# The FFNs' normalised activations, moved 320 bytes along the partition

## The chip, the cores and the metric

One core of one Trainium2 chip. The metric is device time in microseconds (us) for the whole program, weights read from HBM included; the time quoted is the median of three runs. The profile comes from one more execution, taken by the hardware profiler.

## What is computed

Two transformer blocks on 256 tokens of width 1024, all in fp32 (depth 1 each). The first has a mixer over 272 tokens (16 meta tokens in front) and an FFN, the second has an FFN, a mixer and another FFN. What matters here are the three FFNs, each of the form

```python
def swiglu(x, w_in, w_out):
    gate, up = jnp.split(x @ w_in, 2, axis=-1)
    return (jax.nn.silu(gate) * up) @ w_out

x = x + FFN_RESIDUAL_SCALE * rmsnorm_2(swiglu(rmsnorm_2(x, pre), w_in, w_out), post)
```

with an inner width of 2816 (11 groups of 256 columns). In the first block the FFN is the same without the norm behind it and without the factor.

## The kernel before

**Precision.** Every large product is made of three products of fp32r matmuls: weights and activations are each split in a high part and a low part (`whi`, `wlo`; `xn` high, `xn` low), and what is summed in PSUM is whi by high, whi by low and wlo by high.

**Weights.** They come in 129 units of 128 partitions by 2048 values (8192 bytes a partition, 1 MB). SP's queue loads a unit into `raw` (3 slots), ScalarE (line 683) rounds it to `whi`, VectorE (line 1011) makes `wlo` from the two. The tensors `raw`, `whi` and `wlo`, three slots of 8192 bytes a partition each, are allocated one behind the other, and `xa` right behind them. A stationary operand is 128 columns of a unit (512 bytes a partition), so each begins a whole multiple of 512 bytes before the start of `xa`.

**Activations.** `xa` holds 8 times 544 values. For the four norms in front of the three FFNs and of the second mixer, `xn[k]` (k = 0, 1 and 3 for the FFNs, 2 for the mixer) is a view of `xa` in 8 k-tiles of 512 values (2048 bytes): 256 values of high part (one a token), then 256 of low part. The view begins at value `XN_AT[k]`:

```python
XN_AT = (0, 0, 80, 0)
xn = [xa_line[:, c:c + KT * 2 * SEQ].rearrange("p (k c) -> p k c", k=KT) for c in XN_AT]
```

So before the change the FFNs' moving operands begin at the weights' residue modulo 512 bytes, and those of the second mixer 320 bytes past it. ScalarE writes the high parts (line 729), VectorE the low ones (line 1022).

**An FFN on TensorE** (`ffn`, all matmuls issued through the helper `mm`, line 1466). `first_paired_unit` does the first gate unit: per k-tile and 128 columns, whi and wlo by the high part (256 wide), and at the end whi by the low part (256 wide), 48 matmuls. Then `up(0)`, and then ten times a group of gate, up and down:

- `gate`: `hi_products`, 16 matmuls 512 wide (whi by high and low side by side), then `lo_products`, 16 matmuls 256 wide (wlo by high)
- `up`: `lo_products`, then `hi_products`
- `down` (`rows_tile`): 24 matmuls 512 wide, in which the inner activations `hhi`, `hlo` are stationary and the weights move. They do not read `xa`

The last down unit is `rows_last_unit`, from `ya`. In `lo_products` and `hi_products` two matmuls in a row have the same moving operand and two stationary ones.

**The second mixer** uses the same `xa` at 80 values: `first_columns_unit` (48 matmuls 256 wide, in the order of `first_paired_unit`), `columns_tile` (per k-tile whi by high, whi by low, wlo by high, 256 wide) and `tokens_tile` (the activations stationary, the weights moving, 256 wide).

All order is written out by hand; engines meet through semaphores. TensorE waits for a unit's parts (`hi_ready`, `lo_ready`), for the PSUM banks to be read out (`gate_out`, `up_out`) and for the inner activations (`hlo_done`).

Of the kernel before, what the change touches and what calls it, by code (L numbers as in the profile page):

```python
# [45 lines left out]
GROUPS = FF // 256  # L46
UNIT = 2048
SLOTS = 3
XN_AT = (0, 0, 80, 0)
EPS = 1e-6  # L50
NEG = -1e30

# [217 lines left out]
def build_blocks(nc, x_in, meta_in, wstream, ident_in, vecs_in, small_in, const_in, rows_in, out):  # L270
    with ExitStack() as ctx:  # L271
# [146 lines left out]
        neg_sides = exact[:, C_AT["neg_before"][0]:C_AT["neg_after"][0] + P].rearrange("p (a b) -> p a b", a=2)  # L418
        since_r, ones_r = exactly("from"), exactly("ones")
        xa_line = xa[:].rearrange("p k c -> p (k c)")  # L420
        xn = [xa_line[:, c:c + KT * 2 * SEQ].rearrange("p (k c) -> p k c", k=KT) for c in XN_AT]
        ps_line = ps[:].rearrange("p b c -> p (b c)")

# [2 lines left out]
        def vec(name, i=0, n=1):  # L427
            return vecs[:, V_NORM[name] + i:V_NORM[name] + i + n]
# [241 lines left out]
        def _(act):  # L670
# [54 lines left out]
            def hi_of(k, gain, tiles):  # L725

                for kt in tiles:
                    act.wait_ge(norm_turned, KT // 2 + 4 * k + turn_group(kt) + 1)
                    nc.scalar.activation(xn[k][:, kt, 0:SEQ], turn_place(k, kt), ACT.Copy, scale=vec(gain, kt)).then_inc(xa_hi_ready, 1)

            def root_of_x(p, tt):

# [266 lines left out]
        def _(dve):  # L999
# [18 lines left out]
            def norm(k, gain):  # L1018
                for kt in range(KT):

                    dve.wait_ge(xa_hi_ready, KT * (k + 1) + 2 * turn_group(kt) + 2)
                    nc.vector.scalar_tensor_tensor(  # L1022
                        xn[k][:, kt, SEQ:2 * SEQ], turn_place(k, kt), vec(gain, kt),
                        xn[k][:, kt, 0:SEQ].bitcast(F32), ALU.mult, ALU.subtract).then_inc(xa_ready, 1)

                split_ahead(LAST[k])

# [436 lines left out]
        def _(pe):  # L1464
# [26 lines left out]
            def columns_tile(o, slot, a, of, n, skip=0):  # L1491

                for kt in range(KT):
                    w = slice(kt * 256 + a * P, kt * 256 + (a + 1) * P)
                    mm(o, whi[slot][:, w], of[:, kt, skip:n], kt == 0, False)
                    mm(o, whi[slot][:, w], of[:, kt, n + skip:2 * n], False, False)
                    ins = mm(o, wlo[slot][:, w], of[:, kt, skip:n], False, kt == KT - 1)
                return ins

            def first_paired_unit(bank, slot, k):  # L1500

                for kt in range(KT):
                    if k < 2 and kt == 2:
                        pe.wait_ge(x_written, X_BEFORE[k] + len(HALVES))
                        turn_raw(k, range(4, KT), range(TT), True)
                    pe.wait_ge(xa_hi_ready, KT * (k + 1) + kt + 1)
                    for a in range(2):
                        w = slice(kt * 256 + a * P, kt * 256 + (a + 1) * P)
                        mm(ps[:, bank + a, 0:SEQ], whi[slot][:, w], xn[k][:, kt, 0:SEQ], kt == 0, False)
                        mm(ps[:, bank + a, 0:SEQ], wlo[slot][:, w], xn[k][:, kt, 0:SEQ], False, False)  # L1510
                for kt in range(KT):
                    pe.wait_ge(xa_ready, KT * (k + 1) + kt + 1)
                    for a in range(2):
                        w = slice(kt * 256 + a * P, kt * 256 + (a + 1) * P)
                        ins = mm(ps[:, bank + a, SEQ:2 * SEQ], whi[slot][:, w], xn[k][:, kt, SEQ:2 * SEQ], False, kt == KT - 1)
                return ins

            def first_columns_unit(bank, slot, k):

                tiles = [(ps[:, bank, a * SEQ:(a + 1) * SEQ], a * P) for a in range(2)]
                for kt in range(KT):
                    pe.wait_ge(xa_hi_ready, KT * (k + 1) + kt + 1)
                    for o, c in tiles:
                        w = slice(kt * 256 + c, kt * 256 + c + P)
                        mm(o, whi[slot][:, w], xn[k][:, kt, 0:SEQ], kt == 0 and c == 0, False)  # L1530
                        mm(o, wlo[slot][:, w], xn[k][:, kt, 0:SEQ], False, False)
                for kt in range(KT):
                    pe.wait_ge(xa_ready, KT * (k + 1) + kt + 1)
                    for o, c in tiles:
                        w = slice(kt * 256 + c, kt * 256 + c + P)
                        ins = mm(o, whi[slot][:, w], xn[k][:, kt, SEQ:2 * SEQ], False, kt == KT - 1)
                return ins

            def tokens_tile(o, slot, tt):

                hi, lo = slice(tt * P, (tt + 1) * P), slice(SEQ + tt * P, SEQ + (tt + 1) * P)
                for kt in range(KT):
                    w = slice(kt * 256, (kt + 1) * 256)
                    mm(o, xn[2][:, kt, hi], whi[slot][:, w], kt == 0, False)
                    mm(o, xn[2][:, kt, hi], wlo[slot][:, w], False, False)
                    ins = mm(o, xn[2][:, kt, lo], whi[slot][:, w], False, kt == KT - 1)
                return ins

            def rows_tile(slot, a, act_hi, act_lo, first, last):
# [81 lines left out]
            for kind, i in FIRST:  # L1631
# [3 lines left out]
                if kind == "proj":  # L1635
                    n = U_IN + i // 2
                    query = IN_KIND[i][0] == "q"
                    if i == 0:
                        first_unit()
                    if i >= 2:  # L1640
                        pe.wait_ge(lo_ready, n + 1)
                        wait_tiles(pe, i - 2)
                        skip = META if query else 0
                        columns_tile(ps[:, i % 2, skip:TOK], n % SLOTS, i % 2, xa, TOK,
                                     skip).then_inc(unit_used if i % 2 else even_full, 1)
                if kind == "gates":

# [129 lines left out]
            def ffn(f):  # L1777
# [65 lines left out]
            for kind, i in SECOND:  # L1843
                if kind == "munit":
                    n, bank = U_MIX + i, UNIT_BANK[i]
                    pe.wait_ge(lo_ready, n + 1)
                    if i == N_MIX - 1:
                        pe.wait_ge(ml_turn_taken, 3)
                    elif i >= 2:
                        wait_taken(pe, i - 2)  # L1850
                    if i == 0:
                        ins = first_columns_unit(bank, n % SLOTS, 2)
                    elif MIX_KIND[i] == "v":
                        for tt in range(TT):
                            ins = tokens_tile(two(bank)[:, tt, :], n % SLOTS, tt)
                    else:
                        for a in range(2):
                            if (i, a) == (1, 1):

                                pe.wait_ge(mgate_out, 1)  # L1860
                                for tt in range(TT):
                                    c = SEQ + tt * 16
                                    ins = mm(ps[:, 2, c:c + 16], gate_halves[:, tt * P:(tt + 1) * P], vec("gate_sum", 0, 16)[0:BACK + 16, :],
                                             True, True)
                                ins.then_inc(mgate_done, 1)
                            ins = columns_tile(ps[:, bank, a * SEQ:(a + 1) * SEQ], n % SLOTS, a, xn[2], SEQ)
                    ins.then_inc(unit_used, 1)
                if kind == "mgates":
                    spread_rstd(2, 3)
                    pe.wait_ge(gate_w_ready, 1)  # L1870
                    for kt in range(KT):
                        for part in range(2):
                            ins = mm(ps[0:BACK + 16, 2, 0:SEQ], gate_w[:, kt, :], xn[2][:, kt, part * SEQ:(part + 1) * SEQ],
                                     kt == 0 and part == 0, kt == KT - 1 and part == 1)
# [140 lines left out]
```

## Time and profile before

| | |
|---|---|
| median of 3 runs | 797.41 us (797.29 to 797.64) |
| the profiled execution | 797.35 us |
| its span | 795.6 us |
| TensorE matmul busy | 785.1 us (99%), 4710 instructions |
| TensorE weight load busy | 693.8 us (87%) |
| VectorE, ScalarE, GpSimd busy | 533.2, 429.5 and 28.3 us |
| HBM read | 139.69 MB, 177 GB/s over the span |

The span is the time from the program's first instruction to its last; some 1.7 us of the execution lie around it. A matmul's recorded duration is its latency, longer than the step from its start to that of the next, since matmuls overlap: how fast TensorE goes is read from the starts.

### The profile page before, as it was taken

To read this page: it belongs to the slowest core of one execution; us is meant where nothing else is said; L and a number is where in the kernel's file an instruction comes from. 1 tells how busy PE (TensorE), PEld (TensorE's weight loads), DVE (VectorE), ACT (ScalarE), POOL (GpSimd) and SP (SyncE) were. 2 spreads that over 40 slices of the span, in tenths; PEclk is the share of its full clock that TensorE was granted. 3 is DMA by queue.
4 is the path that set the end of the run, shared out by engine and by line. 5 is a ranking of instruction groups with operands and counts; after the bars stand their busy time and mean duration, and the time that the engine had idled before them with its cause. 6 is when DMAs were issued, how large, how long until landed. Compare 5 with 4: busy or idle time off the path is not lost.

```text
span 795.6 us, 12209 instructions
## 1 busy us (share of the span) xinstructions
PE 785.1 (99%) x4710; PEld 693.8 (87%) x4710; DVE 533.2 (67%) x628; ACT 429.5 (54%) x565; POOL 28.3 (4%) x35
## 2 busy tenths in 40 slices
PE   9999999999999999999999999999999999999997
PEld 8989979888888888888888887999988888888885
DVE  7865567766666667866666566766977766666665
ACT  6556658444544548744544446565557644454444
POOL 0000000000000000000000000002420000000000
PEclk9999999999999999999999999999999999999999
DMA  9633333655555543665555554452444655555521
GB/s 335 232 115 117 140 110 139 229 182 187 205 172 203 184 185 110 238 227 192 202 171 208 180 189 158 140 204 108 160 167 165 218 217 175 194 198 175 208 105 54
DMA packets 20797, 141.16 MB, mean 177 GB/s; under 512 B 2448, under 2 KB 2704, under 8 KB 4384
## 3 DMA queue, kind: packets, MB, share of 16 engines
q1 hardware_dynamic: 20192, 138.65, 49.0%
q0 software_dynamic: 576, 2.10, 0.8%
q8 instruction: 21, 0.34, 0.2%
q14 instruction: 8, 0.07, 0.0%
HBM read 139.69 MB, written 1.05 MB: 177 GB/s over the span
## 4 chain that ended last, share of the span: by engine, by line
PE 94%; DVE 2%; ACT 2%; issue 1%; DMA 1%; SPq 0%; DVEq 0%; ACTq 0%
PE ps L1466 93%; ACT whi L683 1%; PE ps L1472 1%; DMA raw<-wstream 1%; DVE x L1215 0%; ACT squared L698 0%; DVE xa L1022 0%; PE ps L1695 0%; DVE wlo L1011 0%; PE ps L1665 0%; PE ps L1915 0%; DVE xg L1210 0%; DVEq L271 0%; ACT L916 0%; PE ps L1697 0%
## 5 line engine op out<-in xcount | busy, mean ns | idle before, releaser
L1466 PE MATMUL ps<-xa,whi 128*128 128x512 f32 (+2 forms) x1744 | 376.1, 346 | 0.0
L1011 DVE TENSOR_TENSOR wlo<-raw,whi 128x2048 fp32r<-128x2048 f32 x128 | 293.7, 2295 | 82.2 <-ACT whi L683 82.1
L1466 PEld LDWEIGHTS ps<-xa,whi 128*128 128x128 f32 x1744 | 300.2, 188 | 40.0 <-issue 2.1
L683 ACT ACTIVATE whi<-raw 128x2048 fp32r<-128x2048 f32 x128 | 244.1, 1908 | 6.9 <-PE ps L1466 6.8
L1466 PE MATMUL ps<-xa,wlo 128*128 128x256 f32 (+1 forms) x1376 | 225.7, 283 | 0.0
L1466 PEld LDWEIGHTS ps<-xa,wlo 128*128 128x128 f32 x1376 | 193.6, 191 | 2.4
L1466 PE MATMUL ps<-whi,hhi 128*128 128x512 f32 x240 | 93.4, 389 | 0.0
L1466 PE MATMUL ps<-wlo,hhi 128*128 128x512 f32 x240 | 93.4, 389 | 0.0
L1466 PE MATMUL ps<-whi,hlo 128*128 128x512 f32 x240 | 93.4, 389 | 0.0
L863 ACT ACTIVATE arena<-ps 128x512 f32<-128x512 f32 x33 | 19.7, 596 | 87.1 <-PE ps L1466 87.1
L877 ACT ACTIVATE hhi<-arena 128x512 fp32r<-128x512 f32 x30 | 19.0, 632 | 88.1 <-PE ps L1466 81.6
L871 ACT ACTIVATE arena<-ps 128x512 f32<-128x512 f32 x33 | 19.7, 596 | 74.1 <-PE ps L1466 74.1
L1466 PE MATMUL ps<-whi,ya 128*128 128x512 f32 x176 | 56.4, 394 | 0.0
L1466 PEld LDWEIGHTS ps<-wlo,hhi 128*128 128x128 f32 x240 | 45.0, 188 | 9.4
L1466 PEld LDWEIGHTS ps<-whi,hlo 128*128 128x128 f32 x240 | 45.0, 188 | 9.4
L1466 PEld LDWEIGHTS ps<-whi,hhi 128*128 128x128 f32 x240 | 45.0, 188 | 9.3
L1257 DVE TENSOR_TENSOR arena<-ps,arena 128x512 f32<-128x512 f32 x33 | 22.8, 691 | 41.1 <-ACT arena L863 41.1
L1266 DVE TENSOR_TENSOR arena<-ps,arena 128x512 f32<-128x512 f32 x33 | 22.8, 691 | 39.3 <-ACT arena L871 39.3
L1278 DVE TENSOR_TENSOR hlo<-arena,hhi 128x512 fp32r<-128x512 f32 x30 | 20.8, 694 | 37.4 <-ACT hhi L877 37.4
L1466 PEld LDWEIGHTS ps<-whi,ya 128*128 128x128 f32 x176 | 33.0, 188 | 6.8
L1466 PE MATMUL ps<-wlo,ya 128*128 128x512 f32 x88 | 34.6, 393 | 0.0
L1466 PE MATMUL ps<-arena 64*128 64x144 f32 (+11 forms) x190 | 23.9, 337 | 1.7 <-DVE arena L1055 1.3
(221 smaller groups left out, 531.5 us busy)
## 6 DMA issues: line engine op xcount, KB each, us to landing
raw<-wstream SPq DMA_DIRECT2D x128, 1024.0 KB, 4.8
gain_row<-rows_in POOLq DMA_DIRECT2D x4, 512.0 KB, 3.9
x<-x_in SPq DMA_DIRECT2D x2, 512.0 KB, 4.0
raw<-wstream SPq DMA_DIRECT2D x2, 512.0 KB, 5.6
out<-x SPq DMA_DIRECT2D x4, 256.0 KB, 2.1
xg<-const_in SPq DMA_DIRECT2D x1, 912.0 KB, 13.0
small<-small_in SPq DMA_DIRECT2D x1, 152.0 KB, 6.0
arena<-meta_in SPq DMA_DIRECT2D x1, 64.0 KB, 4.6
```

The source lines that it names most:

```text
L683: nc.scalar.activation(whi[slot][:], raw[slot][:], ACT.Copy).then_inc(hi_ready, 1)
L863: nc.scalar.activation(silu, products(4)[1], ACT.Copy).then_inc(gate_lo_out, 1)
L871: nc.scalar.activation(up_sum, products(6)[1], ACT.Copy).then_inc(up_lo_out, 1)
L877: nc.scalar.activation(ya[:, 0:2, 0:SEQ] if last else hhi[:], hact, ACT.Copy).then_inc(hhi_done, 1)
L1011: nc.vector.tensor_tensor(wlo[slot][:], raw[slot][:], whi[slot][:].bitcast(F32), ALU.subtract).then_inc(lo_ready, 1)
L1257: nc.vector.tensor_tensor(silu, products(4)[0], silu, ALU.add).then_inc(gate_out, 1)
L1266: nc.vector.tensor_tensor(up_sum, products(6)[0], up_sum, ALU.add).then_inc(up_out, 1)
L1278: nc.vector.tensor_tensor(lo, hact, hi.bitcast(F32), ALU.subtract).then_inc(hlo_done, 1)
L1466: return nc.tensor.matmul(o, lhsT, rhs, start=start, stop=stop, skip_group_check=True)
L1472: ins = nc.tensor.transpose(turn_place(k, kt)[:, tt * P:(tt + 1) * P], x[:, tt, kt * P:(kt + 1) * P], ident[:])
```

## The change

All four views now begin at value 80, so the FFNs' moving operands stand 320 bytes on from where they were, as the mixer's did. The views are cut by part (`xn_hi`, `xn_lo`) instead of by columns; with `XN_HI` all 0 and the distance between the parts `SEQ`, the parts lie beside each other as before, and the 512-wide operand is still 512 values in a row. The order of instructions on every engine, their shapes and their waits stay the same. What differs in the program is the offset of `xa` in the FFNs' instructions: 1152 matmuls 256 wide and 1008 matmuls 512 wide as executed, and the 24 writes of each part on ScalarE and VectorE. (`columns_tile` and `tokens_tile` take their operands in another form, with the same addresses.)

```diff
-XN_AT = (0, 0, 80, 0)
+XN_AT = ((80, SEQ),) * 4
+XN_HI = (0, 0, 0, 0)
...
-        xn = [xa_line[:, c:c + KT * 2 * SEQ].rearrange("p (k c) -> p k c", k=KT) for c in XN_AT]
+
+        xn = []
+        for at, far in XN_AT:
+            line = xa_line[:, at:at + KT * 2 * SEQ if far == SEQ else at + 2 * far]
+            if far == SEQ:
+                xn.append(line.rearrange("p (k h c) -> p k h c", k=KT, h=2))
...
+        xn_hi = [xn[k][:, :, n, :] for k, n in enumerate(XN_HI)]
+        xn_lo = [xn[k][:, :, 1 - n, :] for k, n in enumerate(XN_HI)]
...
-                    nc.scalar.activation(xn[k][:, kt, 0:SEQ], turn_place(k, kt), ACT.Copy, scale=vec(gain, kt)).then_inc(xa_hi_ready, 1)
+                    nc.scalar.activation(xn_hi[k][:, kt, :], turn_place(k, kt), ACT.Copy, scale=vec(gain, kt)).then_inc(xa_hi_ready, 1)
...
-                        xn[k][:, kt, SEQ:2 * SEQ], turn_place(k, kt), vec(gain, kt),
-                        xn[k][:, kt, 0:SEQ].bitcast(F32), ALU.mult, ALU.subtract).then_inc(xa_ready, 1)
+                        xn_lo[k][:, kt, :], turn_place(k, kt), vec(gain, kt),
+                        xn_hi[k][:, kt, :].bitcast(F32), ALU.mult, ALU.subtract).then_inc(xa_ready, 1)
...
-                            ins = mm(ps[:, bank + a, :], whi[slot][:, w], xn[norm][:, kt, 0:2 * SEQ], start and kt == 0, not start and kt == KT - 1)
+                            ins = mm(two(bank + a), whi[slot][:, w], xn[norm][:, kt, :, :], start and kt == 0, not start and kt == KT - 1)
...
-                            ins = mm(ps[:, bank + a, 0:SEQ], wlo[slot][:, w], xn[norm][:, kt, 0:SEQ], start and kt == 0, not start and kt == KT - 1)
+                            ins = mm(ps[:, bank + a, 0:SEQ], wlo[slot][:, w], xn_hi[norm][:, kt, :], start and kt == 0, not start and kt == KT - 1)
```

## Rows read from the trace of the kernel before

**Rows 1.** The page: busy time, share of the span, instructions; the chain that ended last

```profile
PE 785.1 (99%) x4710; PEld 693.8 (87%) x4710; DVE 533.2 (67%) x628; ACT 429.5 (54%) x565; POOL 28.3 (4%) x35
...
PE 94%; DVE 2%; ACT 2%; issue 1%; DMA 1%; SPq 0%; DVEq 0%; ACTq 0%
```

**Rows 2.** What TensorE waited for: us in total, times, longest us

```profile
PE ps L1472 <- DVE x L1215: 2.8, 4, 0.9
PE ps L1466 <- DVE arena L1055: 1.3, 1, 1.3
```

**Rows 3.** TensorE's groups by shape: xcount | busy us, mean ns of one | idle before

```profile
L1466 PE MATMUL ps<-xa,whi 128*128 128x512 f32 x1008 | 240.0, 390 | 0.0
L1466 PE MATMUL ps<-xa,wlo 128*128 128x256 f32 x1264 | 195.2, 282 | 0.0
L1466 PE MATMUL ps<-xa,whi 128*128 128x256 f32 x512 | 93.7, 283 | 0.0
```

**Rows 4.** Timeline of one group of the first FFN: start us, us to last end

```profile
154.64 3.79 PE L1466 MATMUL ps<-xa,whi 128*128 128x512 f32 x16
158.27 4.00 PE L1466 MATMUL ps<-xa,wlo 128*128 128x256 f32 x32
162.10 3.82 PE L1466 MATMUL ps<-xa,whi 128*128 128x512 f32 x16
165.76 0.39 PE L1466 MATMUL ps<-whi,hhi 128*128 128x512 f32 x1
...
171.20 3.79 PE L1466 MATMUL ps<-xa,whi 128*128 128x512 f32 x16
```

**Rows 5.** The first FFN's first units, timeline (offset 0)

```profile
127.48 0.28 PE L1466 MATMUL ps<-xa,whi 128*128 128x256 f32 x1
...
130.12 2.08 PE L1466 MATMUL ps<-xa,whi 128*128 128x256 f32 x16
132.03 2.08 PE L1466 MATMUL ps<-xa,wlo 128*128 128x256 f32 x16
133.96 2.23 PE L1466 MATMUL ps<-xa,whi 128*128 128x512 f32 x9
```

**Rows 6.** The second mixer's first unit, timeline (offset 80)

```profile
498.04 0.28 PE L1466 MATMUL ps<-xa,whi 128*128 128x256 f32 x1
...
501.44 1.98 PE L1466 MATMUL ps<-xa,whi 128*128 128x256 f32 x16
```

**Rows 7.** The second mixer, half of its unit 1, timeline (`columns_tile`, offset 80)

```profile
506.14 0.40 PE L1466 MATMUL ps<-xa,whi 128*128 128x256 f32 x2
...
508.85 0.28 PE L1466 MATMUL ps<-xa,wlo 128*128 128x256 f32 x1
```

**Rows 8.** Matmuls with `xa` in six stretches (by tile): duration ns min/median/max, first and last start

```profile
L1466 PE MATMUL ps<-xa,wlo x29: 278/283/283, 158.3 to 161.6; 128*128 128x256 f32 x29
...
L1466 PE MATMUL ps<-xa,wlo x16: 276/276/276, 497.9 to 501.3; 128*128 128x256 f32 x16
...
L1466 PE MATMUL ps<-whi,xa x29: 281/281/363, 512.9 to 517.9; 128*128 128x256 f32 x29
...
L1466 PE MATMUL ps<-whi,xa x29: 276/276/276, 519.9 to 524.6; 128*128 128x256 f32 x29
...
L1466 PE MATMUL ps<-xa,whi x28: 279/280/280, 532.9 to 537.7; 128*128 128x256 f32 x28
...
L1466 PE MATMUL ps<-xa,whi x15: 389/389/389, 154.6 to 157.8; 128*128 128x512 f32 x15
```

**Rows 9.** Weight loads in three of these stretches, same columns

```profile
L1466 PEld LDWEIGHTS ps<-xa,wlo x28: 188/192/192, 158.4 to 161.6; 128*128 128x128 f32 x28
...
L1466 PEld LDWEIGHTS ps<-xa,wlo x15: 187/188/188, 498.0 to 501.2; 128*128 128x128 f32 x15
...
L1466 PEld LDWEIGHTS ps<-xa,whi x14: 187/188/188, 154.9 to 157.8; 128*128 128x128 f32 x14
```

**Rows 10.** Last matmuls with `ya` before TensorE waits: duration, same columns

```profile
L1466 PE MATMUL ps<-whi,ya x2: 388/388/389, 493.3 to 493.5; 128*128 128x512 f32 x2
```

**Rows 11.** Busy us of engines in the four stretches of rows 4's group, clock, DMA

```profile
core 0: us, PE busy (x) PEld busy (x) DVE busy (x) ACT busy (x) POOL busy (x), PEclk, DMA share, GB/s
...
154.64:158.27 3.63, 3.63 (x18) 3.00 (x16) 1.59 (x2) 2.44 (x2) 0.00 (x0) 1.00 0.80 284
158.27:162.10 3.83, 3.83 (x33) 3.83 (x32) 2.45 (x3) 1.72 (x2) 0.00 (x0) 1.00 0.30 75
162.10:165.76 3.66, 3.66 (x19) 3.01 (x18) 2.62 (x2) 1.20 (x2) 0.00 (x0) 1.00 0.51 215
165.76:171.20 5.44, 5.44 (x26) 4.50 (x25) 3.67 (x3) 2.40 (x2) 0.00 (x0) 1.00 0.51 193
```

**Rows 12.** ScalarE writes the high parts of one norm, timeline

```profile
606.56 3.03 ACT L729 ACTIVATE xa<-ps,vecs 128x256 fp32r<-128x256 f32 x8 [1.35 <-PE ps L1472]
```

More of the change, by code:

```diff
@@ L420, in build_blocks @@
         xa_line = xa[:].rearrange("p k c -> p (k c)")
-        xn = [xa_line[:, c:c + KT * 2 * SEQ].rearrange("p (k c) -> p k c", k=KT) for c in XN_AT]
+        xn = []
[3 more added lines that the diff above has]
+                xn.append(line.rearrange("p (k h c) -> p k h c", k=KT, h=2))
+            else:
+                xn.append(line.rearrange("p (h r) -> p h r", h=2)[:, :, 0:KT * SEQ].rearrange("p h (k c) -> p k h c", k=KT))
+        xn_hi = [xn[k][:, :, n, :] for k, n in enumerate(XN_HI)]
+        xn_lo = [xn[k][:, :, 1 - n, :] for k, n in enumerate(XN_HI)]
+        xa_hi, xa_lo = xa[:, :, 0:TOK], xa[:, :, TOK:2 * TOK]
         ps_line = ps[:].rearrange("p b c -> p (b c)")
@@ L1489, in spread_rstd, with columns_tile @@
                 ins.then_inc(rstd_spread, 1)
-            def columns_tile(o, slot, a, of, n, skip=0):
+            def columns_tile(o, slot, a, of_hi, of_lo, skip=0):
                 for kt in range(KT):
                     w = slice(kt * 256 + a * P, kt * 256 + (a + 1) * P)
-                    mm(o, whi[slot][:, w], of[:, kt, skip:n], kt == 0, False)
-                    mm(o, whi[slot][:, w], of[:, kt, n + skip:2 * n], False, False)
-                    ins = mm(o, wlo[slot][:, w], of[:, kt, skip:n], False, kt == KT - 1)
+                    mm(o, whi[slot][:, w], of_hi[:, kt, skip:], kt == 0, False)
+                    mm(o, whi[slot][:, w], of_lo[:, kt, skip:], False, False)
+                    ins = mm(o, wlo[slot][:, w], of_hi[:, kt, skip:], False, kt == KT - 1)
                 return ins
@@ L1508, in first_paired_unit @@
                         w = slice(kt * 256 + a * P, kt * 256 + (a + 1) * P)
-                        mm(ps[:, bank + a, 0:SEQ], whi[slot][:, w], xn[k][:, kt, 0:SEQ], kt == 0, False)
-                        mm(ps[:, bank + a, 0:SEQ], wlo[slot][:, w], xn[k][:, kt, 0:SEQ], False, False)
+                        mm(ps[:, bank + a, 0:SEQ], whi[slot][:, w], xn_hi[k][:, kt, :], kt == 0, False)
+                        mm(ps[:, bank + a, 0:SEQ], wlo[slot][:, w], xn_hi[k][:, kt, :], False, False)
                 for kt in range(KT):
@@ L1514, in first_paired_unit @@
                         w = slice(kt * 256 + a * P, kt * 256 + (a + 1) * P)
-                        ins = mm(ps[:, bank + a, SEQ:2 * SEQ], whi[slot][:, w], xn[k][:, kt, SEQ:2 * SEQ], False, kt == KT - 1)
+                        ins = mm(ps[:, bank + a, SEQ:2 * SEQ], whi[slot][:, w], xn_lo[k][:, kt, :], False, kt == KT - 1)
                 return ins
@@ L1529, in first_columns_unit @@
                         w = slice(kt * 256 + c, kt * 256 + c + P)
-                        mm(o, whi[slot][:, w], xn[k][:, kt, 0:SEQ], kt == 0 and c == 0, False)
-                        mm(o, wlo[slot][:, w], xn[k][:, kt, 0:SEQ], False, False)
+                        mm(o, whi[slot][:, w], xn_hi[k][:, kt, :], kt == 0 and c == 0, False)
+                        mm(o, wlo[slot][:, w], xn_hi[k][:, kt, :], False, False)
                 for kt in range(KT):
@@ L1535, in first_columns_unit @@
                         w = slice(kt * 256 + c, kt * 256 + c + P)
-                        ins = mm(o, whi[slot][:, w], xn[k][:, kt, SEQ:2 * SEQ], False, kt == KT - 1)
+                        ins = mm(o, whi[slot][:, w], xn_lo[k][:, kt, :], False, kt == KT - 1)
                 return ins
             def tokens_tile(o, slot, tt):
-                hi, lo = slice(tt * P, (tt + 1) * P), slice(SEQ + tt * P, SEQ + (tt + 1) * P)
+                t = slice(tt * P, (tt + 1) * P)
                 for kt in range(KT):
                     w = slice(kt * 256, (kt + 1) * 256)
-                    mm(o, xn[2][:, kt, hi], whi[slot][:, w], kt == 0, False)
-                    mm(o, xn[2][:, kt, hi], wlo[slot][:, w], False, False)
-                    ins = mm(o, xn[2][:, kt, lo], whi[slot][:, w], False, kt == KT - 1)
+                    mm(o, xn_hi[2][:, kt, t], whi[slot][:, w], kt == 0, False)
+                    mm(o, xn_hi[2][:, kt, t], wlo[slot][:, w], False, False)
+                    ins = mm(o, xn_lo[2][:, kt, t], whi[slot][:, w], False, kt == KT - 1)
                 return ins
@@ L1643, in _ @@
                         skip = META if query else 0
-                        columns_tile(ps[:, i % 2, skip:TOK], n % SLOTS, i % 2, xa, TOK,
+                        columns_tile(ps[:, i % 2, skip:TOK], n % SLOTS, i % 2, xa_hi, xa_lo,
                                      skip).then_inc(unit_used if i % 2 else even_full, 1)
@@ L1865, in _ @@
                                 ins.then_inc(mgate_done, 1)
-                            ins = columns_tile(ps[:, bank, a * SEQ:(a + 1) * SEQ], n % SLOTS, a, xn[2], SEQ)
+                            ins = columns_tile(ps[:, bank, a * SEQ:(a + 1) * SEQ], n % SLOTS, a, xn_hi[2], xn_lo[2])
                     ins.then_inc(unit_used, 1)
@@ L1871, in _ @@
                     for kt in range(KT):
-                        for part in range(2):
-                            ins = mm(ps[0:BACK + 16, 2, 0:SEQ], gate_w[:, kt, :], xn[2][:, kt, part * SEQ:(part + 1) * SEQ],
-                                     kt == 0 and part == 0, kt == KT - 1 and part == 1)
+                        mm(ps[0:BACK + 16, 2, 0:SEQ], gate_w[:, kt, :], xn_hi[2][:, kt, :], kt == 0, False)
+                        ins = mm(ps[0:BACK + 16, 2, 0:SEQ], gate_w[:, kt, :], xn_lo[2][:, kt, :], False, kt == KT - 1)
                     ins.then_inc(mgate_halves, 1)
```

## The prediction

> **What bounds the kernel now.** I read the page first. TensorE is busy 99% of the span, the other engines 67% and less, and 94% of the chain that ended last runs through TensorE [rows 1]. The list of TensorE's waits comes next: its longest entries are 2.8 and 1.3 us in 795.6 [rows 2]. The timeline of one FFN group then gives the steps, as differences of starts [rows 4]: the 16 matmuls of gate's `hi_products` take 158.27 - 154.64 = 3.63 us, 227 ns each; the 32 of the two `lo_products` 3.83 us, 119.7 ns each; up's 16 of `hi_products` 3.66 us, 0.03 us more than gate's; the 24 of `down` 5.44 us, 226.7 ns each. Nothing else stands between them: 16.56 us a group, all of it matmul steps.
>
> **What a 256-wide matmul costs at either offset.** At offset 0 the first units show 120.0 ns (22 steps from 127.48 to 130.12) and 120.6 ns for the `lo_products` of `up(0)` (132.03 to 133.96, 16 steps) [rows 5]. At offset 80 the mixer's first unit, which runs through its k-tiles in the same order as `first_paired_unit`, shows 3.40 us for 30 steps, 113.3 ns [rows 6]. The durations say the same: 283 ns against 276 ns [rows 8], and the weight loads beside them 192 ns against 188 ns [rows 9]. But the mixer doesn't always get that: `columns_tile` at the same offset takes 2.71 us for 23 steps, 117.8 ns [rows 7], with durations of 279 to 280 ns. Of the two `tokens_tile` units, equal in all but the slot and the bank, one has 281 ns and the other 276 ns [rows 8]. So offset 80 has two steady paces, 113.3 and 117.8 ns, and which one a stretch falls into isn't set by the offset alone. I take 113.3 for the FFNs, for two reasons: their loops have two stationary operands in a row on one moving operand, as `first_columns_unit` has and `columns_tile` hasn't; and no wait of TensorE precedes them within a group. 117.8 stays as the other end.
>
> **What a 512-wide matmul costs.** The trace has none with `xa` at offset 80; it is the open price of this change. I take no change, 226.7 ns. For it: the weight load beside the 512-wide matmuls already has the undisturbed 188 ns at offset 0 [rows 9]; 226.7 is twice the undisturbed 113.3 of the half width; and the last 512-wide matmuls before a wait of TensorE, with no load behind them, still last 388 ns against 389 [rows 8, 10], so the load costs them next to nothing. Bounds from rows: 6.7 ns less a matmul, if they carry what the 256-wide ones carry (120.0 - 113.3), and 4.5 ns more, if they fall into the slower of the two paces (117.8 - 113.3).
>
> **The sum.**
> - Ten groups in each of three FFNs: 32 x (119.7 - 113.3) = 0.205 us, and the 0.03 us that up's `hi_products` carry over from the disturbed stream before them. 0.235 x 30 = 7.05 us.
> - `up(0)`, three times: 16 x (120.6 - 113.3) + 30 = 147 ns, 0.44 us.
> - `first_paired_unit`, three times: of 48 matmuls some 46 steps at 120.0 - 113.3, 0.31 us, 0.9 us.
> - 1008 matmuls 512 wide [rows 3]: nothing. Of the other rows of that group, 1056 of the 1264 and 96 of the 512 are the 1152 just counted; the rest belong to the mixers and keep their addresses.
> - `down`, the last units, both mixers: not touched.
> - The writes on ScalarE and VectorE at other addresses: nothing. ScalarE makes a k-tile's high part in about 0.36 us (eight in 3.03, of some 0.48 each, overlapped) [rows 12], and TensorE would use one in 4 x 113.3 = 453 ns, instead of 480.
>
> All of it lies on TensorE's path: 8.4 us. Does the cover hold? In the group VectorE is busy 10.3 us and ScalarE 7.8 us of 16.56 (sums of the four stretches, rows 11), and the DMA engines are no more than 0.80 busy in any of them; a group of 16.32 us leaves all of them room, and no new wait comes first. The profiled execution took 797.35 us, 0.06 under the median of the runs, so 797.35 - 8.4 = **789.0 us**.
>
> **The rivals.**
>
> *The slower of the two paces.* The 256-wide matmuls fall to 117.8 ns only. Then 960 x 1.9 + 48 x 2.8 + 138 x 2.2 = 2.3 us, and up to 1.0 us of carry-over: 794.5 us. For it: ten of the second mixer's twelve units run at this pace, with durations of 279 to 281 ns (three of them in rows 7 and 8). Against it: the order of the FFNs' loops, and that gate's `lo_products` come out of a stretch at 226.7.
>
> *The 512-wide ones gain as well.* If an undisturbed matmul costs a fixed 6.7 ns beside its columns, whatever its width, then 226.7 is 213.3 + 6.7 and another 6.7 of disturbance, and 1008 x 6.7 = 6.8 us go too: 782.2 us. For it: 120.0 is 106.7 + 6.7 + 6.7 by the same count. Against it: the 388 ns with no load beside it [rows 10]. If a width costs nothing but its columns, a 512-wide matmul would last 276 + 106.7 = 383 ns, and it lasts 388. In this direction points the Trainium skill, page "TensorE: Matmul & The Clock Gate", section "Back-to-back issue gap", which has 518 cycles for 512 columns, 215.8 ns at 2.4 GHz. By that, an estimate, the 512-wide matmuls would have up to 11 us to give; no stretch of this trace shows them under 226.
>
> *Slower: the 512-wide ones are thrown out of step.* They stream twice as long as the load, and in the whole trace they run undisturbed only where both operands stand at the same residue (`hi_products` and `down` alike). Moved by 320 bytes, each takes the 4.5 ns of the slower pace: 1008 x 4.5 = 4.5 us, in `gate` and `up` of all groups. With the 256-wide ones at 117.8 the sum is 797.35 - 2.3 + 4.5 = 799.6 us, slower. It decides the sign from 2.3 ns a matmul on. Should the 256-wide ones reach 113.3, the same loss leaves 793.4, still faster. Against it: the first 107 ns of such a matmul, in which the load runs, are those of a 256-wide one, and these are undisturbed at offset 80 [rows 6].
>
> *The offset does nothing.* The 113.3 of rows 6 then come from that unit's place in the program (slot 2, one bank, what ScalarE and VectorE do beside it) and not from the 320 bytes: 797.35 us. For it: equal units of the mixer differ by as much [rows 8]. Against it: in the FFNs slots 0, 1 and 2, banks 4 to 7 and all loads on the other engines come by, and the pace is 119.4 to 120.6 everywhere. This is also what the Trainium skill, page "SBUF — State Buffer", section "Who interferes with whom", would have: TensorE has two independent read ports there, for the moving operand and the weight load, and "PE and ACT never wait on anyone". The trace has 276 and 283 ns for one shape, which that rule doesn't explain.
>
> **How the numbers follow.** A measurement of this kernel tells about 0.2%, 1.6 us, from no change. The forecast has 0.50 (788 to 790), the slower pace 0.20, the gain of the 512-wide ones 0.10, their loss 0.10, no effect 0.10. The first three are faster: 0.80; no effect 0.10; slower 0.10. The predicted time is that of the likeliest case. The range leaves out the two cases of the 512-wide matmuls, 0.20 together, and reaches from under the forecast (786.5, should some of the 512-wide ones gain) to no change (797.6).
>
> **What would show it.** Right: one group's `lo_products` x32 take 3.63 us from start to start, with durations of 276 ns and loads of 188; up's `hi_products` 3.63 instead of 3.66; `first_paired_unit` 113.3 ns a step; gate's 16 wide ones 3.63 and `down` 5.44 as before; a group 16.32 us. The slower pace shows as 3.77 us and 279 to 281 ns. The 512-wide matmuls show a loss as 3.70 us for 16 and a gain as 3.52. The prediction is wrong if the 512-wide steps move by more than 1 ns in either direction, if the 256-wide ones stay above 115, or if TensorE's waits grow by the time saved.

## The result, and the profile after

The changed kernel takes 793.92 us (median of 5 runs, 793.66 to 793.95) against 797.64 us (5 runs) for the kernel before: a ratio of 0.995, 95% interval 0.9937 to 0.9963. That is 3.7 us, of the 8.4 us that were forecast (789.0). The sign was right, the size wrong by more than half.

The page of the changed kernel has the same engine shares as [rows 1], with TensorE's busy time down by 3.5 us and the span at 792.0 us (795.6 before):

```profile
PE 781.6 (99%) x4710; PEld 687.9 (87%) x4710; DVE 533.2 (67%) x628; ACT 429.3 (54%) x565; POOL 28.3 (4%) x35
...
PE 94%; ACT 2%; DVE 2%; issue 1%; DMA 1%; SPq 0%; DVEq 0%; ACTq 0%
```

In the steady groups no wait took the time over. What TensorE waited for (us in total, times, longest) is as in [rows 2], with 0.5 us at a place that had 0.3:

```profile
PE ps L1484 <- DVE x L1227: 2.8, 4, 0.9
PE ps L1478 <- DVE arena L1067: 1.3, 1, 1.3
PE ps L1478 <- DVE arena L1101: 0.5, 1, 0.5
```

(Lines stand 12 further down in the changed file: `mm` is at 1478.) The groups by shape (count | busy us, mean ns) already show both signs: against [rows 3] the narrow matmuls with wlo last 5 ns less, the wide ones 2 ns more, and the ones of `down`, which don't read `xa`, have a mean of 390 (389 before).

```profile
L1478 PE MATMUL ps<-xa,whi 128*128 128x512 f32 x1008 | 241.7, 392 | 0.0
L1478 PE MATMUL ps<-xa,wlo 128*128 128x256 f32 x1264 | 189.3, 277 | 0.0
L1478 PE MATMUL ps<-wlo,hhi 128*128 128x512 f32 x240 | 93.5, 390 | 0.0
```

The same group of the first FFN as in [rows 4], timeline, start and length in us:

```profile
154.77 3.84 PE L1478 MATMUL ps<-xa,whi 128*128 128x512 f32 x16
158.45 3.79 PE L1478 MATMUL ps<-xa,wlo 128*128 128x256 f32 x32
162.08 3.82 PE L1478 MATMUL ps<-xa,whi 128*128 128x512 f32 x16
...
171.19 3.84 PE L1478 MATMUL ps<-xa,whi 128*128 128x512 f32 x16
174.87 3.79 PE L1478 MATMUL ps<-xa,wlo 128*128 128x256 f32 x32
```

From start to start: gate's 16 wide matmuls 3.68 us (3.63 before), the 32 narrow ones 3.63 (3.83), up's 16 wide ones with the 24 of `down` 9.11 (9.10). A group takes 16.42 us, not 16.32. The durations (min/median/max) say which kind is disturbed: the narrow ones have the clean 276 ns of [rows 8] throughout, the wide ones now scatter from 388 to 394 where all had 389.

```profile
L1478 PE MATMUL ps<-xa,wlo x28: 276/276/276, 158.6 to 161.6; 128*128 128x256 f32 x28
...
L1478 PE MATMUL ps<-xa,whi x13: 388/392/394, 155.2 to 158.0; 128*128 128x512 f32 x13
```

Where the 0.133 us of a group come from, by the steps from one matmul's start to the next in the steady groups (ns, differences of starts, divided by their count):

| kind | before | after | in a group |
|---|---|---|---|
| 32 narrow, xa by wlo | 119.8 | 113.3 | -206 ns |
| 16 wide of gate, behind `down` | 226.7 | 230.1 | +54 ns |
| 16 wide of up, behind narrow ones | 228.4 | 228.7 | +5 ns |
| 24 of `down` | 226.7 | 227.2 | +13 ns |
| a group | 16553 | 16420 | -133 ns |

27 such intervals make 3.6 us. The first units and the first group of an FFN gain almost nothing (in the first FFN from 127.16 to 154.64 before, from 127.38 to 154.77 after: 0.1 us; 0.1 and 0.0 us in the other two). There the narrow ones of the first group run at 117.8 ns:

```profile
141.85 3.93 PE L1478 MATMUL ps<-xa,wlo 128*128 128x256 f32 x32
```

And `first_paired_unit` is faster, but in the first and the third FFN TensorE then meets a wait that it did not have. `up(0)` needs the `wlo` that VectorE makes meanwhile. Before, VectorE was done with it at 131.80 us (129.52 + 2.28) and TensorE came to it at 132.03 [rows 5]; now VectorE is done at 132.02 and TensorE starts at 132.07, with 0.17 us more in the two steps around that start than at the pace beside them (0.1 us in the third FFN). The list of waits doesn't have it, since matmuls before it are still recorded as running.

```profile
129.52 2.28 DVE L1011 TENSOR_TENSOR wlo<-raw,whi 128x2048 fp32r<-128x2048 f32 x1
```

```profile
129.74 2.28 DVE L1023 TENSOR_TENSOR wlo<-raw,whi 128x2048 fp32r<-128x2048 f32 x1
132.07 2.15 PE L1478 MATMUL ps<-xa,wlo 128*128 128x256 f32 x16
```

(the first before, the other two after.)

In what follows "narrow" is 256 wide, "wide" 512 wide, and paces are such steps, as means over an FFN's groups (gate's wide ones without the first group, which begins with other work; the time of a group from the second on). A pace repeats between the three FFNs of a kernel to 0.1 ns, so one kernel can carry three offsets.

### The profile page after: what moved, and what is told of

It reads as the page before. It is cut to its first block, busy times and chain, and to the rows that moved or that the text cites. A ratio compares the mean times of both kernels' runs of the same rounds, so it can differ in the third digit from the quotient of the medians.

```text
span 792.0 us, 12209 instructions
## 1 busy us (share of the span) xinstructions
PE 781.6 (99%) x4710; PEld 687.9 (87%) x4710; DVE 533.2 (67%) x628; ACT 429.3 (54%) x565; POOL 28.3 (4%) x35
## 4 chain that ended last, share of the span: by engine, by line
PE 94%; ACT 2%; DVE 2%; issue 1%; DMA 1%; SPq 0%; DVEq 0%; ACTq 0%
PE ps L1478 93%; ACT whi L695 1%; PE ps L1484 1%; DMA raw<-wstream 1%; DVE x L1227 0%; ACT squared L710 0%; DVE xa L1034 0%; PE ps L1707 0%; DVE wlo L1023 0%; PE ps L1677 0%; PE ps L1926 0%; DVE xg L1222 0%; DVEq L272 0%; ACT L928 0%; PE ps L1709 0%
## 5 line engine op out<-in xcount | busy, mean ns | idle before, releaser
L1478 PE MATMUL ps<-xa,wlo 128*128 128x256 f32 (+1 forms) x1376 | 219.8, 278 | 0.0
L1478 PEld LDWEIGHTS ps<-xa,wlo 128*128 128x128 f32 x1376 | 187.9, 188 | 2.8
```

What stands on the lines that cost most here:

```text
L1478: return nc.tensor.matmul(o, lhsT, rhs, start=start, stop=stop, skip_group_check=True)
```

## The experiments

All of them start from the changed kernel; short diffs are against it. Before the first I held: **theory F**, that only the first half of a wide matmul, during which the weight load runs, counts; **theory W**, that either half off the weights' residue disturbs it.

### Which half of the wide operand counts

```diff
-XN_AT = ((80, SEQ),) * 4
-XN_HI = (0, 0, 0, 0)
+XN_AT = ((0, 2128), (0, 2048), (80, SEQ), (80, 2048))
+XN_HI = (1, 0, 0, 0)
```

> The parts lie in two blocks, and the 512-wide operand is read as two pieces of 256. First FFN: low part first, at offset 0 from the weights' residue, high part behind it at 80 values. Second FFN: both at 0. Third: both at 80, high first. Mixer as before. Theory F (the weight load runs in the first half of a wide matmul, so only where its first half stands counts): first FFN wide 226.7 ns, narrow 113.3, a group 16.32 us. Theory W (either half off the weights' residue throws the wide ones out of step): first FFN wide 228.7 to 230, narrow 113.3, a group 16.42 or more. In both the second FFN is as the kernel before (narrow 119.8, a group 16.56) and the third as the change (wide 230.1 and 228.7, narrow 113.8, a group 16.44), unless reading in two pieces costs something by itself.

Measured: 797.43 us (kernel before: 797.38). First FFN: wide 232.2 and 233.2 ns, narrow 117.8, a group 16.71 us. Second: 226.7, 228.4, 119.8, 16.55, the kernel before exactly. Third: 230.1, 228.7, 113.8, 16.42, the change exactly. Two pieces cost nothing by themselves, and theory F falls: with the first half at 0 the wide ones are worse than with both at 80. Theory W holds, but it hadn't said that the narrow ones, at the offset of the change and behind disturbed wide ones as there, would lose their 113.3.

```diff
-XN_AT = ((80, SEQ),) * 4
-XN_HI = (0, 0, 0, 0)
+XN_AT = ((0, 2128), (80, 2096), (80, SEQ), (80, SEQ))
+XN_HI = (0, 0, 0, 1)
```

> First FFN: high part first at offset 0, low part at 80. Narrow matmuls read the high part alone, so 119.8 ns in any theory. Theory F: wide 226.7 in gate, a group 16.56 us as before. Theory W: wide 229 and more, a group 16.6 or more. Second FFN: high first at 80, low at 0: narrow 113.3; F gives wide 230.1 and 228.7 as in the change (16.44 us), W something between 226.7 and 230. Third FFN: low part first, both at 80 without a gap: as the change, 16.44 us, in both; if it differs, the narrow ones' residue modulo 2048 bytes counts too.

Measured: 800.41 us. First FFN: wide 232.2 and 233.5, narrow 119.9, a group 16.75. Second: wide 233.2 and 232.8, narrow 117.8, 16.71. Third: as the change, 16.42. Halves at different distances cost more than both at 80, in either order, and the order of the parts alone does nothing.

### Each kind of matmul alone

This is the experiment that the forecast should have been built on: the narrow matmuls read at another offset than the wide ones, with everything else in place (they then read other columns of the same line of `xa`).

```diff
-XN_AT = ((80, SEQ),) * 4
+XN_AT = ((80, SEQ), (0, SEQ), (80, SEQ), (0, SEQ))
+NARROW_AT = (0, 80, 0, 16)
...
+                    c = NARROW_AT[norm]
+                    narrow = xa_line[:, c:c + KT * 2 * SEQ].rearrange("p (k c) -> p k c", k=KT)
...
-                            ins = mm(ps[:, bank + a, 0:SEQ], wlo[slot][:, w], xn_hi[norm][:, kt, :], start and kt == 0, not start and kt == KT - 1)
+                            ins = mm(ps[:, bank + a, 0:SEQ], wlo[slot][:, w], narrow[:, kt, 0:SEQ], start and kt == 0, not start and kt == KT - 1)
```

> The narrow matmuls of the groups read at another offset than the one at which the data lies, so they multiply wrong columns: the FFNs' results are not the reference's. First FFN: wide at 80, narrow at 0. Second: wide at 0, narrow at 80. Third: wide at 0, narrow at 16. Theory S: first narrow 119.8 and wide 230.1 / 228.7, a group 16.63 us; second and third narrow 113.3 and wide 226.7 both times, down 226.7, a group 16.32 us, which is the sum that was forecast. Theory K: in the second and third the narrow ones disturb up's wide ones or fall to 117.8, a group over 16.38.

Measured: 797.83 us (kernel before: 797.46). Together with the two kernels the first two FFNs make a table of two by two, group times in us:

| | narrow at 0 | narrow at 80 |
|---|---|---|
| wide at 0 | 16.553 (before) | 16.493 |
| wide at 80 | 16.733 | 16.420 (the change) |

Added up, the two single steps (-0.060 and +0.180) would give 16.673; together they give 16.420. Neither half of the change is worth what the forecast took it for: the narrow ones alone bring 0.06 us a group, not 0.235, and in the groups at this offset they reach 113.3 only behind disturbed wide ones (and not behind all of those: the narrow ones at 80 behind 232.2 and 233.2 in e1 and e2 run at 117.8). Second FFN, timeline and durations:

```profile
357.48 3.79 PE L1479 MATMUL ps<-xa,whi 128*128 128x512 f32 x16
361.11 3.93 PE L1479 MATMUL ps<-xa,wlo 128*128 128x256 f32 x32
364.88 3.82 PE L1479 MATMUL ps<-xa,whi 128*128 128x512 f32 x16
```

```profile
L1479 PE MATMUL ps<-xa,whi x14: 388/389/390, 357.7 to 360.7; 128*128 128x512 f32 x14
...
L1479 PE MATMUL ps<-xa,wlo x27: 279/280/283, 361.2 to 364.3; 128*128 128x256 f32 x27
```

The wide ones are as before (3.63 us); the narrow ones take 3.77 us, 117.9 ns, with the 279 to 281 ns of the mixer's slower units in [rows 8]. The third FFN (narrow at 16) is the same: 117.9, 16.493. First FFN, wide at 80 and narrow at 0: the wide ones behind `down` take 3.69 us (3.68 in the change), the narrow ones 3.83:

```profile
154.81 3.84 PE L1479 MATMUL ps<-xa,whi 128*128 128x512 f32 x16
158.50 4.00 PE L1479 MATMUL ps<-xa,wlo 128*128 128x256 f32 x32
162.33 3.90 PE L1479 MATMUL ps<-xa,whi 128*128 128x512 f32 x16
```

So the loss of gate's wide ones is their own (230.1 with either kind of narrow ones behind them), and up's wide ones at 80 lose 5 ns more if narrow ones at 0 stand in front (233.5 against 228.7). That each kind goes by its own distance alone (theory S) falls, and of theory K what it says in general stands: the pace of one kind depends on the kind in front of it.

### The same by moving the weights

```diff
+        pad_a = sb("pad_a", [P, 48])
         wlo = [sb(f"wlo{s}", [P, UNIT], F32R) for s in range(SLOTS)]
+        pad_b = sb("pad_b", [P, 16])
         xa = sb("xa", [P, KT, 2 * TOK], F32R)
...
-XN_AT = ((80, SEQ),) * 4
+XN_AT = ((0, SEQ), (0, SEQ), (80, SEQ), (0, SEQ))
```

> The FFNs' views at offset 0 again; wlo alone moved, by 48 values, and xa by 64 behind it, so that narrow matmuls (xa by wlo) have a distance of 64 bytes modulo 256 and the wide ones (xa by whi) a distance of 0. Theory S (each kind of matmul has its own pace by its own distance modulo 256 bytes): narrow 113.3 ns, wide 226.7, as in no kernel so far; a group 16.32 us and, if down is undisturbed, 789 us in all. Theory K (one disturbed kind carries over to the next, through the phase in which loads and matmuls run): down's matmuls with moving wlo are now off its stationary operand's residue, so down goes above 227.5, and gate's wide ones start disturbed; narrow 113.3 or 117.8; a group over 16.4.

Measured: 799.48 us (before: 797.46). Narrow 117.7, gate's wide 229.2, up's 229.6, `down` 229.4, a group 16.61. Each term is on theory K's side: `down`, whose moving wlo now stands 192 bytes off its stationary operand, loses 2.7 ns a matmul, and gate's wide ones, themselves at distance 0, start at 224 to 236 ns and are back at 226.7 after nine. A wide stretch at distance 0 heals; at 80, in the change, its steps go on in turns of 226, 229 and 232 ns to its end. The narrow ones also show whether `xa`'s own address counts or its distance from the weights: `xa` has moved by 256 bytes here, which by itself changes nothing (the table under "Every offset", 64 as 0), and at distance 0 the narrow ones stayed at 119.9 behind disturbed wide ones too (e2, e6). So the 117.7 comes from the distance between `xa` and `wlo`.

### What stands in front of the narrow ones

```diff
-XN_AT = ((80, SEQ),) * 4
+XN_AT = ((0, SEQ), (0, SEQ), (80, SEQ), (0, SEQ))
+NARROW_AT = 80
+SPLIT = (1, 3, None, 8)
...
+                            if bank == 4 and 2 * kt + a >= 2 * KT - SPLIT[norm]:
+                                for h in range(2):
+                                    ins = mm(two(bank + a)[:, h, :], whi[slot][:, w], xn[norm][:, kt, h, :], False, False)
+                                continue
...
+                    c = NARROW_AT
+                    narrow = xa_line[:, c:c + KT * 2 * SEQ].rearrange("p (k c) -> p k c", k=KT)
```

> As the second FFN of e6_split_reads in all three FFNs (wide at 0, narrow reading 80 values on, so the FFNs' results are not the reference's): narrow 117.9 there, coming out of wide ones at 226.7. Here only what stands in front of the narrow ones is changed: the last 1, 3 and 8 wide matmuls of each gate (first, second, third FFN) are issued as two halves of 256 with a weight load each. Theory K (the pace of a narrow stretch is set by the phase in which it is entered): the narrow pace changes between the three FFNs with nothing else changed, to 113.3 in at least one. Theory O (it is set by offset and neighbours alone): 117.9 in all three. The halves themselves cost about 13 ns a split at 120 a half.

Measured: 797.23 us (before: 797.58). The narrow ones run at 117.9 in all three FFNs, as theory O had it; groups take 16.50, 16.53 and 16.59 us. Theory K's forecast missed: two undisturbed or steadily disturbed streams in front (226.7, or 120.0 for sixteen halves) lead to the same 117.9. What e6 and the change differ in is a wide stream whose steps vary (229, 232, 226 ns in turn), and in the groups it is behind such a stream that the narrow ones at this offset have 113.3. That is not enough either: the first group of the change has such a stream in front (its last four steps 230, 231, 226 and 229 ns), and its narrow ones run at 117.8. What decides between the two paces, these runs don't settle.

### The order in the mixer

```diff
-                    mm(o, whi[slot][:, w], of_lo[:, kt, skip:], False, False)
-                    ins = mm(o, wlo[slot][:, w], of_hi[:, kt, skip:], False, kt == KT - 1)
+                    mm(o, wlo[slot][:, w], of_hi[:, kt, skip:], False, False)
+                    ins = mm(o, whi[slot][:, w], of_lo[:, kt, skip:], False, kt == KT - 1)
```

> FFNs as in the change. columns_tile sums whi by high, wlo by high, whi by low, so two stationary operands in a row meet one moving operand. If the order of operands sets the pace at offset 80 (reason one of the prediction), the mixer's units go from 117.8 to 113.3 ns: 9 units x 48 x 4.5 ns = 1.9 us less, 792.0 us. If what counts is how a stretch is entered, they stay at 117.8 and the time at 793.9.

Measured: 793.44 us in one run, which tells no difference from the change; all of the second mixer's columns units stay at 117.8 ns. (The edit reaches the first mixer too, which uses the same helper; its first matmul started 0.35 us earlier in this profiled execution than in that of the change, 11.57 against 11.92 us, so the 0.5 us between the two times need not come from the order.) The order of operands isn't what sets the pace, so the first of my two reasons for 113.3 was none. The change itself says the same: in its second and third FFN `first_paired_unit`, at the offset and in the order of the mixer's first unit, runs at 117.8 ns, and in the first FFN at 113.3; in e7, with the FFNs of the change, the second FFN's has 113.3 too.

### Every offset

```diff
-XN_AT = ((80, SEQ),) * 4
+XN_AT = ((16, SEQ), (32, SEQ), (0, SEQ), (48, SEQ))
```

and so on; six kernels carry eighteen offsets in the FFNs, and six in the mixer.

> Offsets of 16, 32 and 48 values (64, 128 and 192 bytes) in the three FFNs, 0 in the second mixer. Theory of the distance (two streams at the same place at the same time): the mixer's first unit goes from 113.3 to 120 ns, its others from 117.8 to 120; in the FFNs the narrow ones reach 113.3 from some distance on, and the wide ones lose from the same distance on or another. Theory of the place in the program (the mixer's 113.3 has other grounds): the mixer stays at 113.3 and 117.8. I have no number for the wide ones; 16 values may be too few to free the narrow ones (above 117).

> Offsets of 64, 96 and 112 values (256, 384 and 448 bytes) in the three FFNs, 64 in the second mixer. If the wide ones' loss comes only from being off the weights' residue, all three lose as at 80 (gate 230.1, up 228.7 ns). If it depends on the distance, 112 (64 bytes short of the next weight tile's residue) differs from 64. Narrow ones: 113.3 at all three if only nearness to 0 hurts.

> Offsets of 4, 8 and 12 values (16, 32 and 48 bytes) in the three FFNs, 16 (64 bytes) in the second mixer. The mixer is as at 80 if the period is 256 bytes: 113.3 in its first unit, 117.8 in the rest. In the FFNs: if the disturbance of narrow matmuls is a matter of the same 64 bytes, 4, 8 and 12 stay near 120 (or between); if it is one of the same 16 or 32 bytes, they are at 113.3 like 16. The wide ones are at 226.7 as long as the narrow ones are near 120, if both have one cause with opposite sign; a offset with 113.3 and 226.7 together would beat both kernels (789 us).

> Offsets of 20, 24 and 28 values in the three FFNs, 48 in the second mixer. Nothing so far gives these numbers; the pattern of 4, 8, 12, 16, 32 and 48 (narrow 113.9, 117.7, 118.5, 113.8, 118.8, 114.1; wide after down 231.5, 233.5, 233.4, 230.1, 232.8, 233.3 ns) repeats every 64. Theory R (a narrow stretch that comes out of disturbed wide ones falls into its fast pace when the offset is a multiple of 16 or small): 20 as 4, 24 as 8, 28 as 12. An offset whose group takes under 16.43 us beats the change. Mixer at 48: 113.3 in its first unit, 117.8 or less in the rest.

> Offsets of 40, 52 and 60 values in the three FFNs, 32 in the second mixer. Theory R: 40 as 8 (narrow 117.7), 52 as 4 (113.9), 60 as 12 (118.5), wide 231 to 234 in all. An offset just short of the next weight residue (60) may differ from one just past it (4) if the moving stream, which is the faster of the two, runs into the load or away from it. Mixer at 32: between 117.8 and 120, as the FFN's 118.8 at 32.

> Offsets of 36, 44 and 56 values in the three FFNs, 112 in the second mixer. The last open third of the period of 64. If 4.5 ns and more on the wide ones is the rule away from 16, all three groups take over 16.5 us and 16 stays the best; the mixer at 112 is as at 48 (113.3 to 113.8 in its columns units).

They took 799.16, 800.28, 800.39, 800.87, 803.7 and 800.75 us (before: 797.38, 797.38, 797.46, 797.58, 797.58 and 797.65). By offset modulo 64 values (256 bytes), paces in ns, groups in us (the paces of narrow ones and `down` are here means over all ten groups; with the first one left out, its narrow ones at 117.8, offset 16 has the 113.3 and 227.2 of above):

| offset | gate's wide | up's wide | narrow | `down` | group |
|---|---|---|---|---|---|
| 0, 64 | 226.7 | 228.4 | 119.8 | 226.7 | 16.553 |
| 4 | 231.5 | 231.2 | 113.9 | 228.8 | 16.527 |
| 8 | 233.5 | 233.5 | 117.7 | 227.7 | 16.707 |
| 12 | 233.4 | 233.1 | 118.5 | 228.5 | 16.740 |
| 16, 80 | 230.1 | 228.7 | 113.8 | 227.4 | 16.420 |
| 20 | 231.1 | 231.0 | 119.8 | 226.8 | 16.673 |
| 24 | 234.1 | 233.5 | 120.0 | 228.3 | 16.800 |
| 28 | 230.5 | 230.7 | 115.3 | 228.8 | 16.567 |
| 32, 96 | 232.8 | 233.5 | 118.8 | 227.7 | 16.727 |
| 36 | 233.4 | 233.2 | 116.9 | 226.9 | 16.640 |
| 40 | 234.0 | 234.2 | 117.6 | 227.4 | 16.707 |
| 44 | 230.9 | 231.5 | 119.1 | 226.6 | 16.647 |
| 48, 112 | 233.3 | 233.1 | 114.1 | 227.5 | 16.560 |
| 52 | 234.5 | 234.7 | 119.1 | 227.3 | 16.773 |
| 56 | 233.5 | 233.0 | 118.1 | 226.9 | 16.687 |
| 60 | 233.3 | 235.7 | 117.2 | 226.8 | 16.700 |

The offsets with a second value were run at both, with the same paces to 0.1 ns: for these four the period is 256 bytes. Distance alone doesn't order the narrow paces: 16 has 113.8 and 32 is back at 118.8. Theory R, which extended multiples of 16 and "small" ones by a rule, missed (20 isn't like 4, 28 isn't like 12). Every offset but 0 costs the wide ones behind `down` 3.4 to 7.8 ns; 16 is the one with the smallest loss there and the full gain on the narrow ones. Of 16 offsets only 4 and 16 beat 0 at all, going by one profiled execution each. In the mixer the first unit ran at 120.0 ns with offset 0 and the columns units at 119.4 to 120.0 where no wait cuts in, so that the theory of the place in the program is out: same instructions, same slots, other pace. The same by durations, one columns unit at offset 0 (first row, e3) and at 48 (second, e9):

```profile
L1478 PE MATMUL ps<-xa,whi x9: 281/283/389, 551.7 to 555.9; 128*128 128x256 f32 x9
```

```profile
L1478 PE MATMUL ps<-xa,whi x20: 276/276/276, 550.8 to 554.0; 128*128 128x256 f32 x20
```

In this the trace goes against the Trainium skill, page "SBUF — State Buffer", section "Who interferes with whom", by which TensorE's two reads are independent and TensorE never waits on anyone. That would give one pace at every offset, and the trace has 120.0 and 113.3 ns for the same instructions. Where in the chip the two hold each other up, no run here shows.

### Timed versions

```diff
-XN_AT = ((80, SEQ),) * 4
+XN_AT = ((16, SEQ), (16, SEQ), (80, SEQ), (16, SEQ))
```

> The FFNs at 16 values (64 bytes) instead of 80 (320 bytes). Period of 256 bytes: the same paces as the change in every stretch (narrow 113.8, wide 230.1 / 228.7, down 227.4) and the same time, 793.9 us within 0.3. If it is the 320 bytes, another time.

Measured in 5 rounds: 793.93 us (793.61 to 794.03), ratio to the kernel before 0.995 (0.9937 to 0.9964), every pace as in the change. The 320 bytes are 64 bytes.

```diff
-XN_AT = ((80, SEQ),) * 4
+XN_AT = ((80, SEQ), (80, SEQ), (48, SEQ), (80, SEQ))
```

> The change with the second mixer at 48 values instead of 80. By e9_offsets_20_24_28 the mixer's columns units run at 113.3 to 113.8 ns there, not 117.8, and its first unit at 117.8, not 113.3: 9 units x 48 x 4.1 ns = 1.8 us less, 0.2 us more, so 792.3 us, faster than the change (793.9) and than the kernel before (797.5). If the pace in the mixer was set by how the FFN before it left TensorE (it was another offset there), it stays at 117.8 and 793.9.

Measured beside it on the same chip, 5 rounds: 793.87 us (793.27 to 794.52), ratio 0.9951 (0.9937 to 0.9964). Most paces came as expected: seven of the eight columns units behind the two of `tokens_tile` run at 113.3 to 114.0 where no wait cuts in, one at 117.8. The first unit stayed at 113.3, against the 117.8 that e9 has at the same offset, and the second unit of `tokens_tile` went from 113.3 to 117.7. The time did not come as expected. The mixer's last unit ends 1.0 us earlier (576.26 us against 577.25), and then TensorE waits where it hadn't, for VectorE's part of the mLSTM:

```profile
576.26 0.60 PE L1926 MATMUL ps<-ident,arena 128*128 128x128 f32 x4
577.20 0.50 PE L1478 MATMUL ps<-whi,ya 128*128 128x512 f32 x1 [0.34 <-DVE arena L1389]
```

```profile
577.25 0.60 PE L1926 MATMUL ps<-ident,arena 128*128 128x128 f32 x4
577.61 0.48 PE L1478 MATMUL ps<-whi,ya 128*128 128x512 f32 x1
```

(first this kernel, then the change). The third FFN's steady groups begin 0.4 us earlier in its profiled execution, which the runs, 1.2 us apart among themselves, can't tell from nothing. In the mixer other engines follow closely behind TensorE; in the FFNs' steady groups nothing does. No version that I ran can be told from the change as faster.

## Why the prediction was wrong, step by step

- **What bounds the kernel**: right in the steady groups. TensorE's steps are the time there, no new wait came, and the cover held (a group of 16.42 us). The cover was worked out for a group alone: at `up(0)` it was 0.23 us, and in two FFNs a wait for VectorE's `wlo` came.
- **The price of a narrow matmul, 120 against 113.3, and that the FFNs would reach 113.3**: the number was right to 0.1 ns in 27 of 30 groups (0.206 us a group, forecast 0.205), the grounds were wrong. The order of operands doesn't matter (e7), and a stretch that comes out of 226.7 falls into 117.8, not 113.3 (e6). I had even counted "out of a stretch at 226.7" as an argument against the slower pace; behind such a stretch the narrow ones at this distance have it in all 50 groups of e6 and e11 that put them there. That 27 groups reached 113.3 all the same was luck: they did so behind wide matmuls that were disturbed, which the forecast took to be undisturbed.
- **"The 512-wide matmuls: nothing"**: this is the step that failed. It priced their move at zero from rows at offset 0 alone. The 16 behind `down` went from 226.7 to 230.1 ns each, the others from 228.4 to 228.7; that is 54 + 5 ns a group, and `down`, which the forecast had as "not touched", 13 ns by carry-over. That the load beside them lasted an undisturbed 188 ns, and that 388 ns remained without a load, said how they run at offset 0; it said nothing of any other offset, and I used it as if it did. The upper bound, 4.5 ns, holds the measured 3.4.
- **The 0.03 us of carry-over in up's wide ones**: it didn't go. It was put down to the narrow ones in front and would have gone if the wide ones had stayed clean; they show 228.7 (0.3 ns of it new).
- **First units**: forecast 1.3 us with `up(0)`, and 0.7 us for the three first groups; measured 0.09, 0.09 and 0.01 us in the three FFNs for all of it. The first group's narrow ones stay at 117.8 and its wide ones are disturbed; `first_paired_unit` has 113.3 in the first FFN alone, 117.8 in the other two; the 120.6 ns read off for `up(0)` before the change came of the timeline's two decimals (1.920 us for 16 steps, 120.0); and the wait at `up(0)` takes 0.17 us in the first and 0.1 us in the third.
- **The sum**: 8.4 us less 27 x 0.100 (the group's shortfall) less 1.9 us for the first units and groups is 3.8 us. The profiled spans differ by 3.6 and the medians by 3.7; in the profiled execution the first mixer's first matmul starts 0.2 us later than before (11.92 us against 11.69), which is no effect of the edit that anything here shows.
- **The rival that came true** is a mild form of the one called slower: wide ones thrown out of step, narrow ones at 113.3, 793.4 us as worked out there, against 793.9. That the two are so close is chance: it had 144 ns a group for the wide ones, which lost 59, and it knew nothing of what `down`, the carry-over and the first units and groups came to. The time alone would fit the rival of the slower pace as well (794.5); the 113.3 ns of 27 groups rule that one out, though the first groups did as it said. I gave the whole of the disturbed wide ones 0.10. It deserved more: the trace has clean wide matmuls only at equal residues, as the rival itself said, and all 15 other offsets that were tried now say that this isn't chance. That the loss is in the first half, during the load, is refuted by e1 (theory F, and the argument against this rival in the prediction).

## What to carry to other kernels

Where TensorE streams fp32r operands back to back, the distance between the moving operand and the stationary operand in SBUF is worth a sweep, one value per stage of one kernel, over 64 values; here it is worth up to 6% of a 256-wide matmul and 4% of a 512-wide one, with different best values (16 and 0). Don't add up the gains of single kinds of matmul: measure the stage in which they follow each other. And a pace that one unit shows at an address is a pace it can have, not the one it will have.

## What I had not expected of the hardware

- The period of 256 bytes in the distance (64 and 0, 80 and 16, 96 and 32, 112 and 48 values give equal paces).
- Opposite preferences: wide matmuls run at 226.7 ns for whole stretches at distance 0 alone, where narrow ones have one of their worst paces, 119.8.
- Two steady paces at one address and order, 113.3 and 117.8 ns, with the one taken depending on what ran before: at 48 values the mixer's first unit ran at 117.8 in e9 (281 ns) and at 113.3 in e12 (276 ns). The two kernels differ in the offsets of the FFNs alone.
- A disturbance outlives its cause: `down` reads neither `xa` nor a moved operand and still pays up to 2.1 ns a matmul behind a disturbed wide stretch (0.5 in the change, nothing at offset 44).
